# Weight places, the order at the mixer's end, and one modulation part on TensorE

## What is computed

```
mod = silu(c) @ ada_w + ada_b                     # 12 parts of 512: sh1 sc1 gt1 sh2 sc2 gt2
h = rms_norm(x) * (1 + sc1) + sh1 ;  p = h @ w_in
y_a = (layer_norm(wkv7(...)) * lnx_w + lnx_b + bonus * v) * g @ w_out      # recurrence, "a"
y_b, y_c, y_d = gating, short convolution, s5 (y_d = u * sigmoid(v), u, v = gelu(s5) @ glu_w)
x = x + gt1 * ((gates . (y_a, y_b, y_c, y_d)) @ w_o)
x = x + gt2 * (relu(rms_norm(x) * (1 + sc2) + sh2 @ w1)^2 @ w2) ;  x = rms_norm(x)
x = x + attention(x)                               # second block: two kinds of heads, gates, wout
x = x + sum over 8 heads x 16 chosen experts of gate * gelu(x . u_e) * v_e    # rows u_e, v_e gathered
out = rms_norm(x)
```

## Time and profile before

| | us |
|---|---|
| runs | 1535.38 median (1535.05 to 1536.77) |
| profiled execution | 1532.93, of which the span is 1531.6 |
| TensorE busy | 1231.2 (80%) |
| VectorE busy | 938.6 (61%) |
| ScalarE, GpSimd busy | 397.1 (26%), 371.2 (24%) |
| DMA | 488.51 MB, 319 GB/s in the mean; gathered rows 268.45 MB |

### The profile page before, as it was taken

How to read it: one execution, slowest core, us unless ns; L and a number is a source line. 1 busy time by engine, 2 the same in 40 slices (tenths; PEclk the granted TensorE clock), 3 DMA queues, 4 the chain that set the end, 5 groups by cost and what they waited for, 6 DMA issues and landing times.

```text
span 1531.6 us, 14338 instructions
## 1 busy us (share of the span) xinstructions
PE 1231.2 (80%) x4978; PEld 762.0 (50%) x4978; DVE 938.6 (61%) x2022; ACT 397.1 (26%) x1046; POOL 371.2 (24%) x285
## 2 busy tenths in 40 slices
PE   2989999979999899977877647688479787777786
PEld 2876555644676685477544345434265332322332
DVE  6278877945111121157656779998668776777644
ACT  2162111121200122112112132344214433333323
POOL 0001121200000000013323323434236554444430
PEclk9999999979999898998888869788689999999999
DMA  9643334535588665749999999999989999999996
GB/s 369 232 153 123 119 137 172 181 113 200 223 338 334 230 249 197 288 169 419 426 421 424 426 419 415 365 400 421 424 334 394 420 422 421 422 420 421 421 421 273
DMA packets 56377, 488.51 MB, mean 319 GB/s; under 512 B 6512, under 2 KB 8816, under 8 KB 10224
## 3 DMA queue, kind: packets, MB, share of 16 engines
q0 software_dynamic: 36864, 268.45, 42.6%
q1 hardware_dynamic: 18288, 215.55, 36.1%
q10 hardware_dynamic: 1152, 3.59, 0.6%
HBM read 486.51 MB, written 1.05 MB: 318 GB/s over the span
## 4 chain that ended last, share of the span: by engine, by line
PE 48%; DMA 30%; DVE 16%; issue 4%; ACT 2%; POOL 0%; ACTq 0%; DVEq 0%; SPq 0%
PE ps L452 25%; DMA arena<-in_euv,arena 18%; PE ps L816 6%; PE ps L529 6%; PE ps L855 5%; DMA ring<-in_w 5%; DMA ring<-in_euv,arena 5%; PE ps L985 4%; DVE xr L1741 2%; DVE arena L1717 2%; DVE arena L1048 2%; DVE arena L1311 1%; DVE arena L1318 1%; DMA ring<-in_bb 1%; DMA ring<-in_pq 1%
## 5 line engine op out<-in xcount | busy, mean ns | idle before, releaser
L2292 POOL DMA_INDIRECT arena<-in_euv,arena x163 | 208.0, 1276 | 601.4 <-DVE arena L1711 332.1
L452 PE MATMUL ps<-arena,ring 128*128 128x128 f32 (+1 forms) x2320 | 316.1, 300 | 39.1 <-DVE arena L1085 9.8
L452 PEld LDWEIGHTS ps<-arena,ring 128*128 128x128 f32 x2320 | 303.2, 203 | 59.0 <-DVE arena L1079 10.9
L1717 DVE CUSTOM_DVE_ANT_0 arena<-arena 128x1024 f32<-128x1024 f32 x163 | 198.1, 1222 | 87.7 <-DMA arena<-in_euv,arena 87.1
L985 PE MATMUL ps<-arena 128*128 128x512 f32 x356 | 169.1, 619 | 38.1 <-ACT arena L2169 38.1
L855 PE MATMUL ps<-ring,arena 128*128 128x512 f32 x256 | 126.8, 654 | 36.2 <-DMA ring<-in_w 36.2
L2193 ACT ACTIVATE arena<-arena 128x2 f32<-128x2 f32 x127 | 25.7, 203 | 435.3 <-DVE arena L1717 435.2
L985 PEld LDWEIGHTS ps<-arena 128*128 128x128 f32 x356 | 66.8, 194 | 135.9 <-issue 71.9
L816 PE MATMUL ps<-ring,arena 128*128 128x512 f32 x256 | 123.9, 637 | 9.9 <-DVE arena L1079 9.1
L985 PE MATMUL ps<-ring,arena 128*128 128x512 f32 x216 | 106.0, 632 | 31.7 <-ACT arena L2169 31.7
L452 PE MATMUL ps<-arena 128*128 128x128 f32 (+4 forms) x684 | 113.9, 314 | 21.1 <-ACT arena L1830 11.8
(11 more groups left out here) (317 smaller groups left out, 1239.8 us busy)
## 6 DMA issues: line engine op xcount, KB each, us to landing
ring<-in_w SPq DMA_DIRECT2D x32, 2048.0 KB, 12.1
ring<-in_ada SPq DMA_DIRECT2D x12, 2048.0 KB, 8.3
ring<-in_qkv SPq DMA_DIRECT2D x12, 2048.0 KB, 9.3
ring<-in_gates SPq DMA_DIRECT2D x8, 2048.0 KB, 7.8
ring<-in_g SPq DMA_DIRECT2D x8, 2048.0 KB, 8.7
ring<-in_pq SPq DMA_DIRECT2D x8, 2048.0 KB, 10.3
ring<-in_wp SPq DMA_DIRECT2D x5, 2048.0 KB, 8.0
ring<-in_wout SPq DMA_DIRECT2D x4, 2048.0 KB, 9.6
```

Of the source, the lines that this page charges most:

```text
L452: ins = te.matmul(o, l, r, start=(i == 0), stop=(i == len(pairs) - 1))
L1717: ins = v.tensor_tensor_reduce(out=x, in0=x, in1=xn[:, tt, :], scale=1.0, scalar=0.0, op0=ALU.mult, op1=ALU.add, accum_out=hv[:, n % 16:n ...
L2292: gp.indirect_dma_start(slots[i], None, A["euv"], bass.IndirectOffsetOnAxis(ap=idx[:, n // 16 % 4, e % 16:e % 16 + 1].bitcast(U32), axis=0 ...
```

## The change

The ring gets two more places, in the part of the arena that later takes gathered rows, for the tiles from w1 of the first tile to its query projection pq; the first two pq tiles then lie in places 2 to 4, and the order of the first ten row slots follows. In the stream glu comes ahead of part 9 and o_ab 1. Part 2 of the modulation is formed on TensorE as one row, copied by ScalarE and turned by four products of one row. The two norms at the start take their squares first and their roots after. Part 8 is summed ahead of the second half of gates 1. At the mixer's end `glu(0, 0)` and `glu(0, 1)` stand ahead of the layer norm, zA and `merge(0)`, which takes its banks from the other pool; the bonus and the product of lnx_w with g are formed at the fifth doubling of the second tile.

```diff
@@ mixer_order
+                if (i, tt) == (1, 0):
+                    yield "ada", (8,)
+                    open_.append(8)
@@ stream_order
-    names += [("ada", 8), ("o_ab", 1), ("ada", 9), ("glu", 0), ("w_o", 0), ("w_o", 1)]
+    names += [("ada", 8), ("glu", 0), ("ada", 9), ("o_ab", 1), ("w_o", 0), ("w_o", 1)]
@@ the places
-SPOT = [n % RING if n < SECOND else (n - SECOND) % 2 for n in range(len(STREAM))]
+def ring_spots():
+
+    given_up = {("gates", 1): PLACE[("ada", 8)] + 0.5, ("glu", 0): PLACE[("o_ab", 1)] + 0.5}
+    spot, last = [], {}
+    for n, key in enumerate(STREAM):
+        if n < PLACE[("w1", 0, 0)]:
+            places = range(RING)
+        elif n < PLACE[("pq", 0, 0)]:
+            places = range(RING + 2)
+        else:
+
+            places = range(2, RING + 2) if key in (("pq", 0, 0), ("pq", 1, 0)) else range(2)
+        spot.append(min(places, key=lambda i: last.get(i, -1)))
+        last[spot[n]] = given_up.get(key, n)
+    return spot
...
+        def place(i):
+
+            return ring[:, i, :] if i < RING else arena[:, row0 + TILE * (4 - i):row0 + TILE * (5 - i)]
@@ tensor: the start
+            o = take("row2", "misc")
+            te.wait_ge(sig("c_times"), 1)
+            te.wait_ge(*loaded("ada", 2))
+            mm(o[0:1, :], [(cact[:, k:k + 1], weights("ada", 2)[:, k * 512:(k + 1) * 512]) for k in range(8)]
+               ).then_inc(*fill("row2"))
+            spent[("ada", 2)] = full("row2")
...
-            mod_T(2)
+            te.wait_ge(*empty("row2"))
+            o = take("mod2", "misc")
+            for q in range(4):
+                ins = te.matmul(o[:, q:q + 1], mrow[0:1, 0, q * 128:(q + 1) * 128], ones[0:1, 0:1], start=True, stop=True)
+            ins.then_inc(*fill("mod2"))
@@ tensor: the mixer's end
-            for _ in branch["a"]:
-                next(branch["d"], None)
-            merge(0)
-            mod_T(8)
+
+            for _ in range(4):
+                next(branch["a"])
             for _ in branch["d"]:
                 pass
-            pools.update({"main": (0, 1, 2, 3), "misc": (4, 5, 6, 7)})
+            pools["main"] = (0, 1, 2, 3)
...
             glu(0, 0)
             glu(0, 1)
+            for _ in branch["a"]:
+                pass
+            pools["misc"] = (4, 5, 6, 7)
+            merge(0, "misc")
+            mod_T(9)
             glu(1, 0)
-            te.wait_ge(sig("merged"), 2)
+            te.wait_ge(sig("merge_added"), 6)
             rows_T(merged[:, 0, :], "zT0")
             glu(1, 1)
             spent[("glu", 0)] = full("glu0.11")
-            mod_T(9)
@@ vector: the start
-            for tt in range(2):
-                s_ = small[:, 66 + 8 * tt:74 + 8 * tt]
-                norms[0] += 1
-                v.wait_ge(sig("squares"), norms[0])
+            stat = [small[:, 66 + 8 * tt:74 + 8 * tt] for tt in range(2)]
+            for tt, s_ in enumerate(stat):
+                v.wait_ge(sig("squares"), tt + 1)
                 tell(v.tensor_scalar(s_[:, 2:3], s_[:, 0:1], s_[:, 1:2], 1.0 / D, ALU.add, ALU.mult), "mean_square")
-                v.wait_ge(sig("root"), norms[0])
+            mod_T(0, 0)
+            for tt, s_ in enumerate(stat):
+                v.wait_ge(sig("root"), tt + 1)
                 tell(v.reciprocal(s_[:, 4:5], s_[:, 3:4]), "one_over_root")
-            mod_T(0, 0)
-            ada_sum(2)
@@ vector: the recurrence
+                        if (tt, k) == (1, 5):
...
+                            done(v.tensor_tensor(bo8, vr8, bon.unsqueeze(2).broadcast_to([P, 8, 64]), ALU.mult))
...
+                            done(v.tensor_tensor(bonus, bonus, rowa[:, R_LNXB:R_LNXB + 256].unsqueeze(1).broadcast_to(
+                                [P, 2, S]), ALU.add))
+                            after()
+                            done(v.tensor_tensor(bonus, bonus, gr, ALU.mult))
+                            after()
+                            weighed = done(v.tensor_tensor(gr, gr, rowa[:, R_LNXW:R_LNXW + 256].unsqueeze(1)
+                                                           .broadcast_to([P, 2, S]), ALU.mult))
...
+                done(v.tensor_tensor(oo, oo, gr, ALU.mult))
+                after()
+                tell(v.tensor_tensor(oo, oo, bonus, ALU.add), "rwkv_out")
@@ vector: the mixer's end
-            for _ in branch["a"]:
-                next(branch["d"], None)
-            ada_sum(8)
-            merge(0)
-            mod_T(8, 24)
+            next(branch["a"])
             for _ in branch["d"]:
                 pass
-
-
             ada_sum(9)
+            for _ in branch["a"]:
+                pass
...
             glu(0, 0)
             glu(0, 1)
+            merge(0)
+            mod_T(9, 28)
             glu(1, 0)
@@ pool: merge
+                            if tt == 0:
+                                gp.wait_ge(sig("merged"), hf + 1)
@@ sync
                 if BEFORE[n] is not None:
                     sy.wait_ge(*spent[STREAM[BEFORE[n]]])
+                elif SPOT[n] == 3:
+                    sy.wait_ge(*full("o1"))
+                    sy.wait_ge(sig("rwkv_out"), 1)
+                elif SPOT[n] == 4:
+                    sy.wait_ge(*spent[("glu", 0)])
```

More of the change, by code:

```diff
@@ L1101, in vector @@
             v.wait_ge(sig("c_gate"), 1)
[L1102 removed]
+            tell(v.tensor_tensor(cact[:, 0:8], cols[:, C_C:C_C + 8], cact[:, 8:16], ALU.mult), "c_times")
             after()
@@ L1872, in scalar @@
             for tt in range(2):
-                rms(tt, 66, lambda hf: (sig("l_x"), 16))
+                squares(tt, 66, lambda hf: (sig("l_x"), 16))
+            for tt in range(2):
+                root(tt, 66)
+            for tt in range(2):
                 sc.wait_ge(sig("one_over_root"), tt + 1)
                 tell(sc.mul(xn[:, tt, :], xr[:, tt, :], small[:, 70 + 8 * tt:71 + 8 * tt]), "xn_first")
+            sc.wait_ge(*full("row2"))
+            sc.wait_ge(*full("mod0"))
+            emptied(sc.copy(mrow[0:1, 0, :], psum("row2")[0:1, :]), "row2")
             sc.wait_ge(sig("scale1"), 1)
@@ L2037, in scalar @@
                         pass
+            for _ in branch["d"]:
+                pass
             for _ in branch["a"]:
-                next(branch["d"], None)
-            for _ in branch["d"]:
                 pass
```

59 lines of the change are left out of this document (27 added, 32 removed).

## The result

The changed kernel takes 1519.74 us in the median of four runs (1518.41 to 1521.98), the kernel before 1535.22 beside it (1533.42 to 1536.77): a ratio of 0.9901, 95% interval 0.9884 to 0.9918; the medians are 15.5 us apart. The forecast was 1520.3 us, 15.1 us less. A later comparison of the same two gave 0.9917 [0.9899, 0.9936]. The profiled execution took 1518.41, with a span of 1517.1 where before had 1531.6.

A forecast was written before the change was run, and what follows sets the result against it. TensorE was taken to bound up to about 680 us, then full DMA engines as a fixed block; 3.0 (start) + 10.1 (mixer's end) + 2.0 (MLP) = 15.1 us off the 1535.4 median gave 1520.3, range 1511 to 1530.

The forecast's parts named there:

- Row product: At the start on TensorE: 16 one-column records from 22.2 us take 9.4 us, ending at 31.6.
- the rival that it never would: At the start: the one-row product never raises the clock, 4.9 us lost instead of 3.0 gained; 1528.2 us, chance 0.18.
- the one at half rate: At the start: a one-column product runs at half rate, 27.4 us at the low clock; total 1541.8 us, chance 0.05.
- Start, 3.0: Ahead of the first projection: it comes at 38.0 instead of 40.98 us, 3.0 us gained.
- Tail, 10.1: From the recurrence's last products to w_o: glu fills TensorE's wait, w_o at 355.1 instead of 365.23, 10.1 us gained.
- The rival of a slipping recurrence: In the recurrence: ada_sum(8) or the bonus steps delay it, 5.5 us less gain, 1525.8 us; chance 0.12.
- Bonus steps at nothing: Behind the recurrence's fifth doubling on VectorE: four bonus steps, 2.9 us with gaps, fit ahead of the next step, costing nothing.
- MLP, 2.0: First tile's MLP: two extra places remove the two later weight waits, 2.0 us gained; the first wait stays; bounds 0 and 7.4.
- Attention at nothing: Attention and query projections: no wait for a ring tile in them, so nothing gained.
- "A block of fixed length": From the first choice at 681.96 us, full DMA engines make a fixed block; time saved ahead passes to the end one for one.
- a gather near 667: Sign for the profile after: the first gather comes near 667 us.
- "TensorE is busy 34 to 40 of 40 us": Up to about 680 us: TensorE is busy 34 to 40 of 40 us and the DMA engines have room.

The follow-up runs named there:

- in company: New start against old start: in the changed kernel 1519.17 against 1521.91 us; with the final gain's load later and rows let ahead, 1511.61 against 1514.35 us.
- the fourteen traces above: Profiled executions of the kernel before, the changed kernel and the follow-up kernels, compared from first gather to VectorE's addition of the second tile's first product: 195.4 to 202.8 us.
- the mixer's end alone: Kernel before with only the mixer's-end edits, stream order and place rule, three ring places and the old start: 1522.6 us, ratio 0.9925.
- the gain's load later: Changed kernel with the final gain's load moved ahead of the first tile's fourth w1 tile on SyncE's queue: 1511.45 and 1510.32 us.
- the wait: Changed kernel with SyncE waiting for the seventh x_added before loading the second tile's first qkv weights: 1518.75 and 1517.3 us.
- the start alone: Kernel before with only the new start, part 2 as a row product on TensorE and regrouped norms: 1534.22 us, ratio 1.0002.

## Why the prediction was right

The time was 1519.74 where 1520.3 was forecast. The mechanisms were those forecast; the near exactness of the total is partly luck, as two errors cancel. The shift of 18.5 us at the first gather is 2.7 + 11.7 + 0.1 up to the first `up`, 2.5 in the MLP and 1.5 behind it, where 15.1 were forecast; the row phase took 4.0 of them back.

- **Row product: right.** 9.79 us for 9.4, end at 31.9 for 31.6, and 8.41 to 9.79 in the nine traces that have it. The clock rises on a product with one stationary column: 16 records would take 13.7 us at the low level; the rival that it never would (45.8 for the first projection) and the one at half rate (27.4 us for the product) are both out by that row.
- **Start, 3.0: 2.75 at the first projection.** The sums over partitions end at 35.8 for 35.6, and the steps behind them took 2.5 us for 2.4. The projections still begin at the low clock (granted 0.50 from 38 to 40 us). (The prediction's worst case adds up to 45.7 and 4.7 us lost, not 45.8 and 4.9.) What it brings at the end is not settled: alone nothing (ratio 1.0002, interval 2.5 us less to 3.1 more), in company 2.7 us by the medians in both pairs (1521.91 against 1519.17, 1514.35 against 1511.61), whose ranges overlap, or 2.0 and 3.7 us by the ratios. The lead at the first projection isn't lost on the way as a rule, by the fourteen traces above.
- **Tail, 10.1: 11.7.** The term was 1.6 too small: of the 2.2 us set aside for the low clock the glu used 1.1 (8.21 for 16 records, where the merge has 7.10), and some 0.5 are small differences in the other terms. Some of that is where the low clock fell: the recurrence's last 24 records took 0.85 us longer than before, ahead of the tail. The upper bound of 12.3 held.
- **Recurrence: right.** The slack behind part 8 was 1.33 us for 1.2, and the mixer's end alone shows the same 1.33. The rival of a slipping recurrence falls.
- **Bonus steps at nothing: not contradicted.** With the steps back behind the norm zA still doesn't wait, and w_o comes no later (the transposes ahead of it at 346.11 for 346.46). The ratios differ by 0.8 us, which the runs can't tell from nothing; the longer interval of that one trace (2.2 us) goes with waits for rows of 6.6 us behind the load for 5.3.
- **MLP, 2.0: 2.5**, with the first wait kept by the order on SyncE's queue, for the reason named. The run with the load moved shows it: 5.6 us at that place, where 5.4 had been the bound (7.4 less 2.0). In the medians of separate comparisons the line is worth 7.7 to 9.4 (1519.74 and 1519.17 to 1511.45 and 1510.32). The trace of the first has 5.9 at the MLP's end, 3.6 at the first gather, 5.75 at VectorE's addition (the interval is 2.2 shorter, the qkv load having less lead) and 7.1 at the end.
- **Attention at nothing: 1.5 us gained**, at the small products where TensorE was less long at the low clock (mean granted clock from 520 us to the first gather 0.94 for 0.92). How long it is at the low clock differs between executions of one kernel, and the runs give no cause for it.
- **"A block of fixed length": wrong.** The step that the row phase passes the shift on one for one failed: 18.5 us at the first gather became 14.5. It holds only while the second tile's first qkv weights are asked for after VectorE's last wait for rows ahead of the addition. I had read that the DMA share was 1.01 and that the bytes were the same to the end, and took the order of the bytes for given; TensorE's lead let one more tile in ahead of rows that VectorE waited for. It has that lead in six of the seven traces with the two places and without the wait, and in none of the three without the places; how the places bring it isn't shown. The expectation of a gather near 667 was 3.4 late, the row phase took 4.0 back, and the two nearly cancel.
- **"TensorE is busy 34 to 40 of 40 us" up to 680: too simple.** It is 11.35 us in the first 40, 29.32 from 320 to 360 and 31.89 from 640 to 680, the first two of them the places that the change works on; and the DMA engines are short of full in four of the five stretches from 960 to 1160 (340 to 401 GB/s). Neither changes the sum.

The version with the gain's load later beats both kernels: 1511.45 and 1510.32 in two comparisons, ratio to before 0.9856 and 0.9831, some 8 to 9 us below the changed kernel in the medians.

## What to carry to other kernels

A load that waits in an in-order queue holds back every load behind it, so more room for weights buys nothing for a tile that stands behind such a load: read the queue's row just ahead of the late tile. Here the room took away two later waits, 2.5 us, and the larger first one only went when the order was changed. In a stretch where the DMA engines are full, the sum of bytes doesn't fix the time of a point inside it: ask what may now be asked for earlier, and whether the next engine still has waits ahead of it that the early load can lengthen. Here the same load cost nothing behind VectorE's last wait for rows and 2 to 7 us ahead of it. Move work that is ready into a wait before making the wait shorter: that was three quarters of the gain here.

## What was not expected of the hardware

A product with one stationary column costs TensorE about as much as a full one and also brings its clock up: 16 records in 9.79 us from 22.12 on (8.41 to 9.79 in nine traces), where 16 full ones behind an idle stretch took 9.25 before and 10.08 with the start alone; the transposes behind take 1.97 for 16, and the sum over partitions 1.05 where it took 1.87. The Trainium skill, in TensorE: Matmul & The Clock Gate, "③ FILL", has the time go by the moving columns alone; the trace agrees for one column.

The low clock is not the same in two executions of one kernel: the gain's load later had its first gather at 659.84 and at 662.59, with nothing but the execution between them, and the start alone ran from 1528.6 to 1542.26. Twelve runs of it against 23 of before still left 2.8 us to either side, as much as the start was meant to bring.
